# Products behind six norms start from the high parts alone, and a third weight panel is mixed into four of them

## Chip, cores and metric

The kernel runs on one core of one Trainium2 chip. The metric is the device time of one execution in microseconds, the median of three runs. Times from the trace are microseconds (us) of one profiled execution.

## What is computed

Two transformer blocks of depth 2 in a row, on 512 tokens of width 1024 (and 256 context tokens in the first block), all in float32 with float32 accuracy:

```python
# first block, for each of two layers (mixer A, then mixer B)
h  = rmsnorm(x, g) * (1 + scale) + shift      # likewise hc from the context
x  = x + gate * mixer(h, hc)
...
x  = rmsnorm(x, final_g)                      # norm "nf"
# second block, for each of two layers
y = rms_norm(h, nw[0])                        # norm "s00" (layer 0), "s10" (layer 1)
y = even_mixer(y) if layer == 0 else odd_mixer(y)
h = h + rms_norm(y, nw[1])                    # post norm "s01", "s11"
y = conv_ffn(rms_norm(h, nw[2]))              # norm "s02", "s12"
h = h + rms_norm(y, nw[3])                    # post norm "s03", "s13"
```

A `conv_ffn` is two products of 1024 x 2816 (`u`, `v`), a causal convolution of width 3 over `u`, `gelu(conv) * v`, and a product back to 1024.

## The kernel before

**Split products.** TensorE multiplies in a format with fewer mantissa bits than float32. Each operand is split in two parts of that format, `high = round(a)` and `low = a - high`, and a product is made of three: high x high, high x low, low x high (`split_product`, lines 364 to 366). For an activation the parts are `HH` and `HL`, in eight chunks k of 128 rows by 512 tokens; for a weight they are `WH` and `WL`. A weight panel is 1024 rows by 128 columns, eight chunks as well, so a panel with one output bank takes 24 matmuls of 512 columns.

**Who does what.** SyncE loads raw panels into three slots `raww`, in the order of use. ScalarE writes `WH` (`ahead`, line 307, instruction on line 316), GpSimd subtracts and writes `WL` (`split_low`, instruction on line 1449). There are three slots of `WH`/`WL` (`SPLIT = 3`, line 31): the high part of a panel can be written only after the last product of the panel three before it. All engines work strictly in program order, so `ahead` and `split_low` stand at places written out by hand in each engine's program, and a wait there holds everything behind it. The panels behind a norm are numbered here 0, 1, 2, 3 and so on in their order of use.

**The norms that the change touches.** Norms `n0` and `n1` (first block) scale before the product: VectorE makes `SQ` (line 2343), ScalarE rounds it into `HH` (lines 2097, 2098), VectorE subtracts into `HL` (line 2354), and signals `h_made`. The four "late" norms `s00`, `s02`, `s10`, `s12` multiply the product's result by the reciprocal root afterwards, so that products can start before the sum of squares is known. For each chunk k:

- VectorE finishes the residual `XC` chunk k. Behind a post norm this is `post_norm` (line 2363): L2368 scales `y` (mark `ynormed`), L2373 adds it to `XC` (mark `x_made`), L485 (`late_low`) makes `HL`. The loop is skewed: in step k it scales chunk k, adds chunk k-1, makes the low part of chunk k-2. For `s00` the loop is another (L2277, then `late_low` of chunk k-1), which the change leaves alone.
- ScalarE (`late_parts_act`, line 462) waits for `x_made`, writes `HH` chunk k (L466) and the square of the chunk into one of four places of `TMP` (L470). From k = 4 on the square waits for `statted[st, 3]`, TensorE's use of the first four squares, and the high parts of the later chunks stand behind it in the queue.
- TensorE (`lin_pair`, line 1555) takes two panels at once: for each k it waits for `h_made` (the low part) and issues the three products for each panel. After k = 3 and k = 7 it sums four squares (`square_group`, line 441, eight matmuls L447).

Behind the pair TensorE takes panel 2 by itself (`lin`, 24 matmuls), then `late_stat` (line 451, eight matmuls L455 of one column), which waits for ScalarE's copy of the sums (L472, mark `ss`), then panel 3, then `late_spread` (L515). This is so in `even_pe` (panels `e_f` 0 to 3), `ffn_pe` (`up_u` 0, `up_v` 0, `up_u` 1, `up_v` 1) and `odd_pe` (`o_k` 0 to 3). On ScalarE the copy `ss` is the last line of `late_parts_act`; the next line of its program is `ahead(act, ..., 4)`, which writes the high parts of panels 3 and 4 (`ffn_act`, line 2138, and the like in the other stages). The high part of panel 2 is written before the norm. GpSimd's low parts follow the high parts in order.

**PSUM banks** for products are handed out in turn, seven of them (`lin_bank`), and `claim` waits for the last reader of a bank.

## Time and profile before

| | us |
|---|---|
| median of 3 runs | 2239.02 (2236.71 to 2241.35) |
| profiled execution | 2237.86 |
| its span, first to last instruction | 2235.9 |
| TensorE busy | 2096.1 (94% of the span) |
| VectorE, ScalarE, GpSimd busy | 1042.0, 883.7, 724.7 |
| mean granted TensorE clock | 0.973 of full |

The time of a run holds the span and some 2 us around it. The page's fourth part follows the chain of work that ended last back through the engines: 82% of it is TensorE, 8% VectorE, 4% ScalarE. Its second part has a line PEclk, the clock that TensorE was granted in tenths of full speed. It is below 9 in three of the 40 slices, of 56 us each. A busy TensorE at half clock does half the work.

In the rows below, a name such as `L364` is a line of the kernel; `x8` behind a row is the number of instructions merged into it; the part in brackets is how long the engine had been idle, and whom it waited for.

### The profile page before, as it was taken

To read this page: it belongs to the slowest core of one execution; us is meant where nothing else is said; L and a number is where in the kernel's file an instruction comes from. 1 tells how busy PE (TensorE), PEld (TensorE's weight loads), DVE (VectorE), ACT (ScalarE), POOL (GpSimd) and SP (SyncE) were. 2 spreads that over 40 slices of the span, in tenths; PEclk is the share of its full clock that TensorE was granted. 3 is DMA by queue.
4 is the path that set the end of the run, shared out by engine and by line. 5 is a ranking of instruction groups with operands and counts; after the bars stand their busy time and mean duration, and the time that the engine had idled before them with its cause. 6 is when DMAs were issued, how large, how long until landed. Compare 5 with 4: busy or idle time off the path is not lost.

```text
span 2235.9 us, 29867 instructions
## 1 busy us (share of the span) xinstructions
PE 2096.1 (94%) x11466; PEld 1641.1 (73%) x11466; DVE 1042.0 (47%) x1722; ACT 883.7 (40%) x1636; POOL 724.7 (32%) x424
## 2 busy tenths in 40 slices
PE   5999999999999998998889999998998899999997
PEld 4888655788665645987667888886986677888886
DVE  3521887432466623377436434333127616625353
ACT  4322666433566723534443222234117723323222
POOL 1331122433000012240234444453444452444443
PEclk9999999999999999798989999999999999999999
DMA  7221333132000012220123333332331031333332
GB/s 282 66 67 57 105 100 91 48 104 72 14 1 1 1 48 65 67 87 28 41 64 94 104 94 93 102 89 76 95 95 34 25 104 50 110 94 92 106 90 71
DMA packets 255889, 169.16 MB, mean 76 GB/s; under 512 B 5776, under 2 KB 247159, under 8 KB 254599
## 3 DMA queue, kind: packets, MB, share of 16 engines
q1 hardware_dynamic: 252512, 158.55, 23.9%
q0 software_dynamic: 2192, 8.45, 1.2%
q8 instruction: 94, 1.54, 0.3%
q10 hardware_dynamic: 1047, 0.26, 0.1%
q14 instruction: 44, 0.36, 0.0%
HBM read 165.10 MB, written 2.14 MB: 75 GB/s over the span
## 4 chain that ended last, share of the span: by engine, by line
PE 82%; DVE 8%; issue 4%; ACT 4%; POOL 1%; DMA 0%; ACTq 0%; DVEq 0%; POOLq 0%
PE ps L364 20%; PE ps L366 20%; PE ps L365 20%; PE ps L542 6%; PE ps L650 5%; PE ps L614 3%; PE ps L1551 2%; PE ps L593 1%; DVE PT L632 1%; DVE MX L555 1%; POOL WL L1449 1%; DVE NB L552 1%; PE ps L982 1%; PE ps L515 1%; ACT PB L567 1%
## 5 line engine op out<-in xcount | busy, mean ns | idle before, releaser
L1449 POOL TENSOR_TENSOR WL<-raww,WH 128x1024 fp32r<-128x1024 f32 (+2 forms) x239 | 563.4, 2362 | 890.8 <-ACT WH L316 885.6
L364 PE MATMUL ps<-HH,WH 128*128 128x512 f32 (+1 forms) x1368 | 526.4, 385 | 31.6 <-DVE HL L485 19.5
L365 PE MATMUL ps<-HL,WH 128*128 128x512 f32 (+1 forms) x1368 | 521.0, 381 | 0.0
L366 PE MATMUL ps<-HH,WL 128*128 128x512 f32 (+1 forms) x1368 | 520.3, 380 | 0.0
L316 ACT ACTIVATE WH<-raww 128x1024 fp32r<-128x1024 f32 (+2 forms) x239 | 245.6, 1034 | 327.7 <-PE ps L366 327.6
L364 PEld LDWEIGHTS ps<-HH,WH 128*128 128x128 f32 x1368 | 261.2, 191 | 91.4 <-issue 28.0
L366 PEld LDWEIGHTS ps<-HH,WL 128*128 128x128 f32 x1368 | 260.6, 190 | 49.3
L365 PEld LDWEIGHTS ps<-HL,WH 128*128 128x128 f32 x1368 | 261.3, 191 | 46.9
L567 ACT ACTIVATE PB<-ps,NB 128x256 f32<-128x256 f32 (+5 forms) x256 | 168.1, 657 | 99.8 <-DVE NB L556 49.3
L614 PE MATMUL ps<-ident,PB 128*128 128x128 f32 x952 | 154.4, 278 | 11.6 <-DVE PT L632 7.1
L650 PE MATMUL ps<-PT,ARENA 128*64 128x512 f32 (+3 forms) x688 | 131.7, 490 | 10.0 <-ACT PT L634 6.5
L364 PE MATMUL ps<-f_h,WH 128*128 128x512 f32 x352 | 137.7, 391 | 1.6 <-DVE f_l L2571 1.6
L366 PE MATMUL ps<-f_h,WL 128*128 128x512 f32 x352 | 137.1, 389 | 0.0
L365 PE MATMUL ps<-f_l,WH 128*128 128x512 f32 x352 | 137.0, 389 | 0.0
L552 DVE TENSOR_REDUCE NB<-ps 128x1 f32<-128x768 f32 (+4 forms) x128 | 92.5, 723 | 93.2 <-PE ps L542 91.7
L614 PEld LDWEIGHTS ps<-ident,PB 128*128 128x128 f32 x952 | 108.7, 143 | 21.9 <-DVE PT L632 12.6
L634 ACT ACTIVATE PT<-ps 128x256 f32<-128x256 f32 (+1 forms) x192 | 83.7, 436 | 89.4 <-PE ps L614 87.2
L2384 DVE TENSOR_TENSOR ARENA<-ps,ARENA 128x512 f32<-128x512 f32 x60 | 40.9, 690 | 157.8 <-PE ps L366 131.0
L2558 DVE SCALAR_TENSOR_TENSOR ARENA<-ARENA,COL 128x511 f32<-128x511 f32 x44 | 110.8, 2519 | 1.6
L2147 ACT ACTIVATE ARENA<-ARENA 128x512 f32<-128x512 f32 x44 | 27.8, 632 | 172.9 <-DVE ARENA L2560 172.9
L555 DVE TENSOR_REDUCE MX<-ps 128x1 f32<-128x512 f32 (+3 forms) x128 | 74.1, 579 | 42.4 <-PE ps L542 42.0
L632 DVE COPY PT<-ps 128x384 f32<-128x384 f32 (+2 forms) x192 | 91.3, 476 | 3.2 <-PE ps L614 2.1
(324 smaller groups left out, 3344.1 us busy)
## 6 DMA issues: line engine op xcount, KB each, us to landing
raww<-in_ffn_w_up SPq DMA_DIRECT2D x88, 512.0 KB, 3.8
raww<-in_ada_w SPq DMA_DIRECT2D x32, 512.0 KB, 3.6
raww<-in_ffn_w_down SPq DMA_DIRECT2D x32, 448.0 KB, 3.7
raww<-in_odd_w_in SPq DMA_DIRECT2D x24, 512.0 KB, 3.7
raww<-in_even_w_in SPq DMA_DIRECT2D x21, 512.0 KB, 3.7
raww<-in_a_w_in SPq DMA_DIRECT2D x20, 512.0 KB, 3.8
raww<-in_ffn_w_down SPq DMA_DIRECT2D x16, 512.0 KB, 3.9
ADA<-in_ada_w SPq DMA_DIRECT2D x6, 1024.0 KB, 16.4
```

The costliest lines, as they stand in the source:

```text
L316: nc.scalar.activation(parts_of(k)[0], raw_slot(k), ACT.Copy).then_inc(*split_hi.mark(k))
L364: nc.tensor.matmul(out, lh, rh, start=start and k == ks[0], stop=False)
L365: nc.tensor.matmul(out, lh, rl, start=False, stop=False)
L366: ins = nc.tensor.matmul(out, ll, rh, start=False, stop=stop and k == ks[-1])
L542: ins = nc.tensor.matmul(ps[:, bk, c0 % 512:c0 % 512 + w], lhs, rhs, start=(q == 0), stop=(q == len(ms) - 1), skip_group_check=True)
L552: nc.vector.tensor_reduce(nb, score_span(A, r, i), AX_X, ALU.max, negate=True)\
L567: nc.scalar.activation(PB[:, t % 4, 0:job["tiles"][i]["n"] * P], score_span(A, r, i), ACT.Exp, bias=NB[:, r % 4, i:i + 1], scale=A["scale" ...
L614: ins = nc.tensor.transpose(ps[:, b, q * P:(q + 1) * P], PB[:, t % 4, (first + q) * P:(first + q + 1) * P], ident[:, :])
L632: nc.vector.tensor_copy(dst, src).then_inc(*pt_dve.mark(*key))
L650: ins = nc.tensor.matmul(ps[p0:p0 + HD, 7, a:z], v, PT[at][:, blk, q0_ + a:q0_ + z], start=(q == 0), stop=(q == n - 1), skip_group_check=True)
L1449: nc.gpsimd.tensor_tensor(lo, raw_slot(k), hi.bitcast(F32), ALU.subtract).then_inc(*split_lo.mark(k))
L2558: chain(dve, dve_step, nc.vector.scalar_tensor_tensor(c[:, 1:S], u[:, 0:S - 1], col(cw, 22 + m), c[:, 1:S], ALU.mult, ALU.add))
```

## The change

In `lin_pair` TensorE waits for the high part of chunk k (`act_out["hh", ...]`), issues the two products that use it for each panel, then waits for the low part (`h_made`) and issues the third. For the four late norms a third panel (panel 2) is mixed in: its chunks 0 to 3 follow the pair's chunks 1 to 4, its chunks 4 to 7 follow the pair's chunk 7. `square_group(..., 1)` stands behind all three panels, and `late_stat` right behind that. In `late_parts_act` all eight high parts come ahead of the squares 4 to 7. In `post_norm` the skew is one step less: the loop scales chunk k, makes the low part of chunk k-1, waits for the scaled chunk k and adds it. `ahead`, `split_low`, `late_stat`, `square_group` and the order of the panels stay as they are.

```diff
--- before.py
+++ after.py
@@ -465,8 +465,10 @@
                 act.wait_ge(*ready(k))
                 nc.scalar.activation(HH[:, k, 0:S], XC[:, k, 0:S], ACT.Copy, scale=col("norm_w_2", 8 * w + k))\
                     .then_inc(*act_out.mark("hh", st, k))
-                if k >= 4:
-                    act.wait_ge(*statted[st, 3])
+                if k < 4:
+                    nc.scalar.activation(TMP[:, k, :], XC[:, k, 0:S], ACT.Square).then_inc(*squared.mark(st, k))
+            act.wait_ge(*statted[st, 3])
+            for k in range(4, 8):
                 nc.scalar.activation(TMP[:, k % 4, :], XC[:, k, 0:S], ACT.Square).then_inc(*squared.mark(st, k))
             act.wait_ge(*statted[st, 7])
             nc.scalar.activation(TMP[:, 0, :], bank(("ss", st)), ACT.Copy).then_inc(*act_out.mark("ss", st))
@@ -1552,26 +1554,49 @@
                 ins.then_inc(*grouped.mark(*gk))
             last_use(key, *gk)
 
-        def lin_pair(pe, two, h_, segs, ready, st=None):
-
-            outs = []
-            for stage, key, m, reader_of in two:
-                pe.wait_ge(*split_lo[key,])
+        def lin_pair(pe, two, h_, segs, norm, st=None, third=None):
+
+            def claimed(stage, key, m, reader_of):
                 for name, r0, nr in segs:
                     b = lin_bank((stage, m, name))
                     claim(pe, b, reader_of(m, name))
-                    outs.append((stage, key, m, name, r0, nr, b))
-            for k in range(8):
-                pe.wait_ge(*ready(k))
+                    yield stage, key, m, name, r0, nr, b
+
+            def step(outs, k, low_made=None):
                 for stage, key, m, name, r0, nr, b in outs:
                     wh, wl = parts_of(key)
-                    ins = split_product(ps[:, b, 0:nr], lambda k: (wh[:, k, :], wl[:, k, :]), h_(r0, nr), [k],
-                                        k == 0, k == 7)
+                    hh, _ = h_(r0, nr)(k)
+                    nc.tensor.matmul(ps[:, b, 0:nr], wh[:, k, :], hh, start=(k == 0), stop=False)
+                    nc.tensor.matmul(ps[:, b, 0:nr], wl[:, k, :], hh, start=False, stop=False)
+                if low_made:
+                    pe.wait_ge(*low_made)
+                for stage, key, m, name, r0, nr, b in outs:
+                    wh, _ = parts_of(key)
+                    _, hl = h_(r0, nr)(k)
+                    ins = nc.tensor.matmul(ps[:, b, 0:nr], wh[:, k, :], hl, start=False, stop=(k == 7))
                     if k == 7:
                         ins.then_inc(*grouped.mark(stage, m, name))
-                if st and k % 4 == 3:
-                    square_group(pe, st, k // 4)
-            for stage, key, m, _ in two:
+
+            outs, late, late_k = [], [], 0
+            for one in two:
+                pe.wait_ge(*split_lo[one[1],])
+                outs += claimed(*one)
+            for k in range(8):
+                pe.wait_ge(*act_out["hh", norm, k])
+                step(outs, k, h_made[norm, k])
+                if third and 1 <= k <= 4:
+                    if k == 1:
+                        pe.wait_ge(*split_lo[third[1],])
+                        late += claimed(*third)
+                    step(late, late_k)
+                    late_k += 1
+                if st and k == 3:
+                    square_group(pe, st, 0)
+            for k in range(late_k, 8 if third else 0):
+                step(late, k)
+            if st:
+                square_group(pe, st, 1)
+            for stage, key, m, _ in two + ([third] if third else []):
                 last_use(key, stage, m, segs[-1][0])
 
         def lin_rows(pe, stage, name, c, nn, tiles, reader):
@@ -1599,7 +1624,7 @@
         def mixer_a_pe(pe):
             lin_pair(pe, [("ak", ("a_k", m), m,
                            lambda m, s: (act_out, ("raw", "ak", m)) if s == "lat" else (act_out, ("akc", m)))
-                          for m in range(2)], h_at, BOTH, lambda k: h_made["n0", k])
+                          for m in range(2)], h_at, BOTH, "n0")
             lin_rows(pe, "av", "a_v", 0, 256, range(6), lambda t: (act_out, ("av", t)))
             for m in range(8):
                 lin(pe, "aq", ("a_q", m), m, h_at, BOTH,
@@ -1615,7 +1640,7 @@
 
             lin_pair(pe, [("ckv", ("b_ckv", 0), 0, lambda m, s: (act_out, ("ckv", s))),
                           ("kr", ("b_kr", 0), 0, lambda m, s: (act_out, ("kr", s)))], h_at, BOTH,
-                     lambda k: h_made["n1", k])
+                     "n1")
             for m in range(2):
                 lin(pe, "cq", ("b_cq", m), m, h_at, LAT, lambda m, s: (act_out, ("cq", m)))
 
@@ -1655,11 +1680,9 @@
 
         def even_pe(pe):
             lin_pair(pe, [("ef", ("e_f", m), m, lambda m, s: (dve_out, ("efr", m))) for m in range(2)], h_at, LAT,
-                     lambda k: h_made["s00", k], "s00")
-            for m in range(2, 4):
-                lin(pe, "ef", ("e_f", m), m, h_at, LAT, lambda m, s: (dve_out, ("efr", m)))
-                if m == 2:
-                    late_stat(pe, "s00")
+                     "s00", "s00", ("ef", ("e_f", 2), 2, lambda m, s: (dve_out, ("efr", m))))
+            late_stat(pe, "s00")
+            lin(pe, "ef", ("e_f", 3), 3, h_at, LAT, lambda m, s: (dve_out, ("efr", m)))
             late_spread(pe, "s00")
             lin_rows(pe, "ev", "e_v", 0, P, range(4), lambda t: (act_out, ("ev", t)))
             for i in range(2):
@@ -1812,12 +1835,13 @@
                 if what == "up" and i == 0:
                     lin_pair(pe, [(f"u{l}", ("up_u", l, 0), 0, lambda m, s: (dve_out, ("u", l, m))),
                                   (f"v{l}", ("up_v", l, 0), 0, lambda m, s: (dve_out, ("prod", l, m)))], h_at, LAT,
-                             lambda k: h_made[before, k], before)
+                             before, before,
+                             (f"u{l}", ("up_u", l, 1), 1, lambda m, s: (dve_out, ("u", l, m))))
+                    late_stat(pe, before)
                     continue
                 if what == "up":
-                    lin(pe, f"u{l}", ("up_u", l, i), i, h_at, LAT, lambda m, s: (dve_out, ("u", l, m)))
-                    if i == 1:
-                        late_stat(pe, before)
+                    if i > 1:
+                        lin(pe, f"u{l}", ("up_u", l, i), i, h_at, LAT, lambda m, s: (dve_out, ("u", l, m)))
                     lin(pe, f"v{l}", ("up_v", l, i), i, h_at, LAT, lambda m, s: (dve_out, ("prod", l, m)))
                     if i == 1:
                         late_spread(pe, before)
@@ -1844,11 +1868,10 @@
 
         def odd_pe(pe):
             lin_pair(pe, [("ok", ("o_k", m), m, lambda m, s: (dve_out, ("ok", m))) for m in range(2)], h_at, LAT,
-                     lambda k: h_made["s10", k], "s10")
-            for m in range(2, 8):
+                     "s10", "s10", ("ok", ("o_k", 2), 2, lambda m, s: (dve_out, ("ok", m))))
+            late_stat(pe, "s10")
+            for m in range(3, 8):
                 lin(pe, "ok", ("o_k", m), m, h_at, LAT, lambda m, s: (dve_out, ("ok", m)))
-                if m == 2:
-                    late_stat(pe, "s10")
                 if m == 3:
                     late_spread(pe, "s10")
             for i in range(4):
@@ -2363,17 +2386,17 @@
         def post_norm(dve, st, w, nxt):
             norm_recip(dve, st, 4)
             dve.wait_ge(*rinv_made[st, 0])
-            for k in range(10):
+            for k in range(9):
                 if k < 8:
                     nc.vector.scalar_tensor_tensor(y_of[st][:, k, :], y_of[st][:, k, :], col("norm_w_2", 8 * w + k),
                                                    bank(("rinv", st, 0)), ALU.mult, ALU.mult)\
                         .then_inc(*dve_out.mark("ynormed", st, k))
-                if 1 <= k < 9:
-                    dve.wait_ge(*dve_out["ynormed", st, k - 1])
-                    nc.vector.tensor_tensor(XC[:, k - 1, 0:S], XC[:, k - 1, 0:S], y_of[st][:, k - 1, :], ALU.add)\
-                        .then_inc(*x_made.mark(st, k - 1))
-                if k >= 2:
-                    late_low(dve, nxt, k - 2, w + 1)
+                if k >= 1:
+                    late_low(dve, nxt, k - 1, w + 1)
+                if k < 8:
+                    dve.wait_ge(*dve_out["ynormed", st, k])
+                    nc.vector.tensor_tensor(XC[:, k, 0:S], XC[:, k, 0:S], y_of[st][:, k, :], ALU.add)\
+                        .then_inc(*x_made.mark(st, k))
             late_recip(dve, nxt)
 
         def late_scaled(dve, dst, key, done, st, by=None):
```

## Rows read from the trace of the kernel before

**Rows 1.** Page, parts 1 and 2: busy us of each engine; granted TensorE clock in tenths.

```profile
PE 2096.1 (94%) x11466; PEld 1641.1 (73%) x11466; DVE 1042.0 (47%) x1722; ACT 883.7 (40%) x1636; POOL 724.7 (32%) x424
...
PEclk9999999999999999798989999999999999999999
```

**Rows 2.** Waits of TensorE, whole run: us in total, times, longest us.

```profile
PE ps L364 <- DVE HL L485: 19.5, 8, 5.0
...
PE ps L364 <- DVE HL L2354: 7.8, 2, 4.1
...
PE ps L364 <- POOL WL L1449: 3.9, 5, 1.5
```

**Rows 3.** Timeline, norm n1: start us, us, engine, line, what, count, [idle before, releaser].

```profile
492.23 0.49 ACT L2098 ACTIVATE HH<-SQ,MODS 128x256 fp32r<-128x256 f32 x1
...
494.05 0.76 PE L364 MATMUL ps<-HH,WH 128*128 128x512 f32 x1 [3.66 <-DVE HL L2354]
```

**Rows 4.** Timeline, first products behind norm s02.

```profile
1149.91 1.41 DVE L2368 SCALAR_TENSOR_TENSOR ARENA<-ARENA,COL,ps 128x512 f32<-128x512 f32 x2 [2.17 <-PE ps L515]
1151.23 0.69 DVE L2373 TENSOR_TENSOR XC<-XC,ARENA 128x512 f32<-128x512 f32 x1
...
1151.95 0.72 ACT L466 ACTIVATE HH<-XC,COL 128x512 fp32r<-128x512 f32 x1 [4.42 <-DVE XC L2373]
...
1153.10 0.74 DVE L485 SCALAR_TENSOR_TENSOR HL<-XC,COL,HH 128x512 fp32r<-128x512 f32 x1
...
1153.98 0.77 PE L364 MATMUL ps<-HH,WH 128*128 128x512 f32 x1 [4.12 <-DVE HL L485]
...
1155.02 0.74 DVE L485 SCALAR_TENSOR_TENSOR HL<-XC,COL,HH 128x512 fp32r<-128x512 f32 x1
...
1155.68 0.74 DVE L2368 SCALAR_TENSOR_TENSOR ARENA<-ARENA,COL,ps 128x512 f32<-128x512 f32 x1
```

**Rows 5.** Timeline, norm s02 behind the first four squares, chunk 5.

```profile
1164.56 0.75 DVE L485 SCALAR_TENSOR_TENSOR HL<-XC,COL,HH 128x512 fp32r<-128x512 f32 x1 [1.77 <-ACT HH L466]
...
1165.37 0.50 PE L364 MATMUL ps<-HH,WH 128*128 128x512 f32 x1 [0.56 <-DVE HL L485]
```

**Rows 6.** Timeline, norm s02 from the last four squares to the fourth panel.

```profile
1169.67 1.06 PE L447 MATMUL ps<-TMP,ones 128*32 128x512 f32 x8
...
1170.80 0.60 ACT L472 ACTIVATE TMP<-ps 128x512 f32<-128x512 f32 x1 [3.48 <-PE ps L447]
...
1172.43 4.75 POOL L1449 TENSOR_TENSOR WL<-raww,WH 128x1024 fp32r<-128x1024 f32 x2 [24.05 <-ACT WH L316]
...
1176.25 0.95 PE L455 MATMUL ps<-oned,TMP 128*128 128x1 f32 x8
...
1177.05 0.49 PE L364 MATMUL ps<-HH,WH 128*128 128x512 f32 x1
```

**Rows 7.** Timeline, first products behind norm s00.

```profile
864.88 7.45 POOL L1449 TENSOR_TENSOR WL<-raww,WH 128x1024 fp32r<-128x1024 f32 x3 [8.12 <-ACT WH L316]
...
870.25 0.76 PE L364 MATMUL ps<-HH,WH 128*128 128x512 f32 x1 [4.96 <-DVE HL L485]
```

**Rows 8.** Timeline of TensorE, one-column products with a wait among them, between 512-column ones.

```profile
534.17 1.39 PE L417 MATMUL ps<-oned,SQ 128*128 128x1 f32 x12
536.53 2.02 PE L417 MATMUL ps<-oned,SQ 128*128 128x1 f32 x16 [0.96 <-ACT SQ L395]
```

**Rows 9.** Stretches: us, busy us (count) of each engine, granted clock, DMA share, GB/s.

```profile
538.20:541.63 3.43, 3.43 (x11) 2.75 (x11) 0.00 (x0) 2.95 (x4) 0.00 (x0) 0.50 0.00 0
1153.98:1159.44 5.46, 5.46 (x13) 4.30 (x14) 5.46 (x9) 3.42 (x6) 0.00 (x0) 0.50 0.00 0
1845.68:1848.93 3.25, 3.25 (x8) 2.57 (x9) 3.25 (x6) 1.89 (x4) 0.00 (x0) 0.50 0.02 5
903.50:927.30 23.80, 23.80 (x114) 23.80 (x113) 5.68 (x15) 9.26 (x15) 4.22 (x3) 0.50 0.08 23
```

**Rows 10.** Timeline, entry of the e_v products.

```profile
902.55 0.30 PE L364 MATMUL ps<-WH,HH 128*128 128x128 f32 x1 [2.27 <-DVE ARENA L2384]
```

## The prediction

> **What bounds the kernel now.** I read the page's busy line first: TensorE is busy for 94% of the span, no other engine for half of it [rows 1]. What matters is therefore which stretches of TensorE's work move, where it stands still, and at which clock it runs. The list of TensorE's waits comes next: 19.5 us in eight waits for the low parts of the late norms and 7.8 us in two for those of n0 and n1 [rows 2]. These ten waits are the most that the change can touch. They are not all the low part's fault. Then I read the timeline at each norm. Behind s02 the first scaling starts at 1149.91, the sum is there at 1151.92, the high part at 1152.67, the low part at 1153.84, and the first product starts at 1153.98 [rows 4]. A second, short wait stands behind the first four squares, at chunk 5: 0.56 us, because the high part of chunk 5 stood behind a square on ScalarE [rows 5]. Last I read what happens between the last squares and panel 3, where the change takes work away [rows 6], and the granted clock of stretches, since TensorE comes out of these waits at 1.2 GHz: 13 products in 5.46 us, 0.42 us each, against 0.23 us at 2.4 GHz (24 products between the end of L447 at 1170.73 and 1176.25) [rows 6, 9].
>
> **Norms n0 and n1.** VectorE's and ScalarE's work stays; the first product waits for the high part. In n1 that ends at 492.72; with the 0.14 us from the end of a part to its product (1153.84 to 1153.98 in [rows 4]) TensorE starts at 492.86 and not at 494.05 [rows 3, 4]. Gain 1.2 us. n0 has the same two steps and a wait as long [rows 2], so 2.4 us for both. The same three products per panel and chunk are issued in another order: no cost. TensorE gets one wait more per chunk, 48 in all. At most chunk borders of today it passes a satisfied wait, and the list of waits shows no time for them, so I take nothing; the upper bound is 0.11 us each (a first product after a wait takes 0.50 us and not 0.39 [rows 5]), 5 us in all.
>
> **Head of the three post norms (s02, s10, s12).** Today the first high part is the third link: two scalings, one addition. In the changed order it is scaling 0.74, addition 0.69, high part 0.72, with 0.03 us between engines (1151.92 to 1151.95) and 0.14 to TensorE: 2.35 us behind 1149.91, against 4.07 today [rows 4]. Gain 1.7 us each. The new order on VectorE is slower per chunk, though. Today a cycle takes 1.92 us (low part at 1153.10, the next at 1155.02). Now the low part of a chunk waits for the high part of the same chunk and holds up the next addition: 0.68 + 0.03 + 0.72 + 0.03 from the start of an addition to the start of the low part, 0.66 more to the next addition (1155.02 to 1155.68), 2.1 us [rows 4]. The last low part is there 18.0 us behind 1149.91. TensorE still needs 2 + 12 products and the squares after it, 4.3 us, so it can't be done before 22.3; by its own work it is done 26.3 us behind today (1176.25), less the gains here, 23.9. The supply does not bind, but it caps the gain at 4.0 us where the clock should rise early. Panel 2 covers this: with it a chunk costs 9 x 0.23 = 2.1 us, the pair alone 1.4.
>
> **Chunk 5 (all four late norms).** The high parts run ahead of the squares, so the wait of 0.56 us and the 0.11 us of its first product go: 0.7 us each [rows 5]. The squares 4 to 7 come later on ScalarE but still before panel 2 is done: nothing.
>
> **Head of s00.** Here two low weight parts have to be ready. Three take 7.45 us from 864.88, so the second is there near 869.85; the first product starts at 870.25 today and at 869.95 then: 0.3 us [rows 7]. Panel 2's low part ends at 872.3, before TensorE is through chunk 1.
>
> **Panel 3: a new wait.** This term decides. Today the chain behind the last squares is: L447 at 1169.67, copy of the sums on ScalarE 1170.80, behind it in ScalarE's queue the high part of panel 3, then GpSimd's low part from 1172.43, the first of two in 4.75 us, so until 1174.80 [rows 6]. Meanwhile TensorE does panel 2's 24 products (5.5 us) and the eight small ones of L455, so it never waits for that chain. The change moves those 24 products ahead of the squares and leaves the chain as it is, hanging on the squares. Now L455 waits for the copy (end 1.73 us behind the start of L447, where L447 ends at 1.06), and panel 3 waits for its low part, 5.14 us behind it; with the step to TensorE 5.2. Today's distance from L447 to panel 3 is 1177.05 - 1169.67 = 7.4, of which 5.5 is panel 2. So 5.2 stands where 1.9 would be: +3.3 us at each of four norms, +13.2 us. Who else waits: on TensorE everything; the low part of panel 4 and the later ones keep their distance to panel 3 and have slack. I see no bound much below this, since each link is a queue order that the diff doesn't touch; 2.9 to 3.6.
>
> **The clock in the new wait.** TensorE now has 512-column products, then 0.7 us of nothing, 0.8 us of one-column products and 2.6 us of nothing. The nearest row is a stretch from 534.17 to 538.4 with only one-column products and a wait of 0.96 us; behind it the clock was 1.2 GHz for 3.4 us [rows 8, 9]. At half speed 3.4 us cost 1.7. Low stretches elsewhere last 3.25 to 5.46 us [rows 9]. I take 1.7 at each, +6.8; bounds 0 and 2.7. The Trainium skill speaks for the lower bound: its page "TensorE: Matmul & The Clock Gate", section "Why this matters for your kernels", only warns of idle gaps longer than either piece here. By it the clock stays and this term is nothing. The trace does not agree, as the stretch at 534 had no longer gap. The same page, Part 1, says that the number of slow products varies from run to run of one kernel; that agrees with the 3.25 and 5.46 us here, and is why I use a mean at the heads: starting 1.7 us earlier in the low state may give 0.85, or up to 3.4 where the rise comes a step earlier.
>
> **Banks.** Panel 2 now takes the bank before the sum of squares and not after. In the even stage the last bank that the e_v products claim is then read by the third of four L2384 and not the second, some 0.6 us later, on top of the wait of 2.27 us [rows 10]: +0.6. In the other stages these readers are long done.
>
> **Sum.** -2.4 (n0, n1) -5.1 (three heads) -0.3 (s00) -2.8 (chunk 5) +13.2 +6.8 +0.6 = +10.0 us. The profiled execution took 2237.9, so 2247.9; the median of the three runs is 1.1 above it, so 2249.0. Later waits (for instance 3.9 us for GpSimd's parts [rows 2]) hang on late_spread, which moves along, so nothing absorbs the shift.
>
> **Rivals.** (B) The stall is there, the clock stays up: 2249.0 - 6.8 = 2242.2, no measurable change. For it: the two idle pieces are short, and this is what the skill's rule above would give. Against it: [rows 8, 9].
> (C) Not slower, by the clock at one place: the e_v products run at 1.2 GHz for 23.8 us behind the wait of 2.27 us [rows 9, 10]. Should the clock stay up there, half of that, 11.9, comes back: 2237. It decides if the clock does not fall in 902 to 904. Against it: the wait before it grows by 0.6, and the work that follows is the same 128-column kind.
> (D) Panel 3's parts are ready by another way and only the gains are left: -10.6 + 0.6, 2229. That needs a high part ahead of the copy of the sums on ScalarE, which the order of its program forbids; it would also be the case if I misread that order.
> (E) The 48 added waits cost 0.11 us each and low stretches last longer: 2254 and above. Against it: the satisfied waits of today.
>
> **Chances.** Forecast 0.60 (2245 to 2254 with the bounds of head, clock and stall), B 0.15, C 0.08, D 0.08, E 0.09. A measurement of this kernel can tell about 0.2%, 4.5 us. D is faster (0.08); B and C are the same (0.23); forecast and E slower (0.69). The range takes in the forecast, B and most of C, and leaves out D and half of E: 2238 to 2254.
>
> **What would show it.** Right: TensorE's waits for L485 and L2354 shrink from 27.3 us by some 12; new waits of L455 for L472 (0.7 us, four) and of L364 for L1449 (2.6 us, four) appear; low clock behind each; VectorE's cycle is 2.1 us. Wrong: panel 3's first product less than 5 us behind the last L447, or a granted clock of 1.00 through these stretches, or e_v products at 2.4 GHz.

## The result, and the profile after

The changed kernel takes 2254.99 us (median of 4 runs, 2251.12 to 2256.05), the kernel before 2239.39 us beside it: ratio 1.0064, 95% interval 1.0049 to 1.0078, so 15.6 us slower. The forecast was 2249.0, 10 us slower. The median lies 1 us above the upper end of the range. The profiled execution took 2254.13 us; its span is 2252.2 us against 2235.9 before, 16.3 more.

TensorE's waits of the changed kernel, whole run (us in total, times, longest; late_low is now L487, the low weights L1451, the copy of the sums L474, the products of a pair L1569, L1570 and L1576):

```profile
PE ps L364 <- POOL WL L1451: 13.0, 9, 2.3
...
PE ps L1569 <- ACT HH L466: 7.2, 3, 2.4
...
PE ps L1569 <- ACT HH L2121: 5.4, 2, 3.0
PE ps L1569 <- POOL WL L1451: 4.5, 1, 4.5
...
PE ps L364 <- ACT TMP L1892: 3.6, 1, 3.6
PE ps L455 <- ACT TMP L474: 3.2, 4, 0.8
...
PE ps L364 <- DVE ARENA L2407: 2.9, 1, 2.9
```

The 27.3 us of waits for low parts in [rows 2] are now 17.1 us, for high parts and, at s00, for a low weight panel (7.2 + 5.4 + 4.5). In return the wait of L364 for GpSimd's weights rose from 3.9 to 13.0 us, and a new wait of 3.2 us stands ahead of L455. Of both kinds one new wait stands at the same place of each late norm. Timeline at the head of s02, which answers to [rows 4]:

```profile
1161.69 0.75 DVE L487 SCALAR_TENSOR_TENSOR HL<-XC,COL,HH 128x512 fp32r<-128x512 f32 x1
...
1161.80 0.77 PE L1569 MATMUL ps<-HH,WH 128*128 128x512 f32 x1 [2.41 <-ACT HH L466]
...
1163.83 0.75 DVE L487 SCALAR_TENSOR_TENSOR HL<-XC,COL,HH 128x512 fp32r<-128x512 f32 x1
```

The first product no longer waits for the low part, and VectorE's cycle is 2.14 us for a chunk (1161.69 to 1163.83). Timeline behind the last squares of s02 (start us, us, engine, line; idle before and its releaser in brackets), which answers to [rows 6]:

```profile
1181.41 1.06 PE L447 MATMUL ps<-TMP,ones 128*32 128x512 f32 x8
1182.55 0.60 ACT L474 ACTIVATE TMP<-ps 128x512 f32<-128x512 f32 x1 [3.79 <-PE ps L447]
1183.04 1.99 ACT L316 ACTIVATE WH<-raww 128x1024 fp32r<-128x1024 f32 x2
1183.29 1.02 PE L455 MATMUL ps<-oned,TMP 128*128 128x1 f32 x8 [0.81 <-ACT TMP L474]
1184.16 4.68 POOL L1451 TENSOR_TENSOR WL<-raww,WH 128x1024 fp32r<-128x1024 f32 x2 [26.28 <-ACT WH L316]
...
1186.57 0.79 PE L364 MATMUL ps<-HH,WH 128*128 128x512 f32 x1 [2.26 <-POOL WL L1451]
```

Follow one release after another: squares on TensorE, copy on ScalarE, high weights behind it in ScalarE's queue, low weights on GpSimd, product on TensorE. Between the squares and that product TensorE has only the eight small products of L455 in its program, so it stands still for the rest of the chain. From the squares to the fourth panel (the prediction's panel 3) it is 5.16 us.

Four stretches of the changed kernel, with the columns of [rows 9]: behind that stall, the rest of the panel, behind s00's stall, and the entry of the e_v products. The column in front of the last two numbers is the granted clock:

```profile
1186.30:1189.71 3.41, 3.14 (x8) 2.48 (x8) 0.32 (x2) 0.00 (x0) 3.41 (x3) 0.50 0.52 148
1189.72:1193.50 3.78, 3.78 (x18) 3.13 (x17) 0.00 (x0) 0.00 (x0) 1.47 (x1) 1.00 0.69 201
...
896.10:902.90 6.80, 5.91 (x14) 4.65 (x15) 0.94 (x2) 0.00 (x0) 3.29 (x3) 0.50 0.65 203
909.80:933.60 23.80, 23.80 (x114) 23.80 (x114) 5.06 (x13) 8.21 (x13) 3.17 (x3) 0.50 0.08 23
```

The clock is 1.2 GHz (0.50) behind the stall of s02 for 3.4 us, and behind that of s00 for 6.8.

The next table lays out each late norm by stages: from the spread that precedes it to the first product of the pair, on to L455, to the fourth panel, and to the norm's own spread. Times are us, between starts in TensorE's timelines of both kernels. In both, the stretch to L455 holds 72 products and both groups of squares; in the changed kernel it also holds the new wait of 0.81.

| norm | to the first product | to L455 | to the fourth panel | to its spread | sum |
|---|---|---|---|---|---|
| s00 | 6.12, now 5.64 | 22.59, now 20.98 | 0.81, now 3.28 | 5.58, now 8.38 | +3.16 |
| s02 | 6.19, now 4.49 | 22.26, now 21.49 | 0.81, now 3.28 | 5.58, now 7.02 | +1.44 |
| s10 | 5.81, now 4.49 | 22.03, now 21.97 | 0.81, now 3.28 | 5.59, now 7.18 | +2.69 |
| s12 | 6.19, now 4.49 | 21.36, now 21.70 | 0.81, now 3.28 | 5.58, now 7.15 | +2.67 |

The four norms make +10.0 us of the +16.3. Of the rest, 3.0 us are there before s00 begins and 3.4 come between s00 and s02.

### The profile page after: what moved, and what is told of

Its sections match the earlier page's. It is cut to its first block, busy times and chain, and to the rows that moved or that the text cites. A ratio compares the mean times of both kernels' runs of the same rounds, so it can differ in the third digit from the quotient of the medians.

```text
span 2252.2 us, 29867 instructions
## 1 busy us (share of the span) xinstructions
PE 2110.1 (94%) x11466; PEld 1653.9 (73%) x11466; DVE 1052.4 (47%) x1722; ACT 883.7 (39%) x1636; POOL 723.1 (32%) x424
## 3 DMA queue, kind: packets, MB, share of 16 engines
HBM read 165.10 MB, written 2.14 MB: 74 GB/s over the span
## 4 chain that ended last, share of the span: by engine, by line
PE 74%; issue 12%; DVE 7%; POOL 3%; ACT 3%; DMA 0%; ACTq 0%; DVEq 0%; POOLq 0%
PE ps L364 17%; PE ps L365 17%; PE ps L366 17%; PE ps L544 6%; PE ps L652 5%; PE ps L616 3%; POOL WL L1451 2%; PE ps L1553 2%; PE ps L595 1%; DVE PT L634 1%; DVE MX L557 1%; POOL ACC L378 1%; DVE NB L554 1%; PE ps L984 1%; ACT PB L569 1%
## 5 line engine op out<-in xcount | busy, mean ns | idle before, releaser
L1451 POOL TENSOR_TENSOR WL<-raww,WH 128x1024 fp32r<-128x1024 f32 (+2 forms) x239 | 562.6, 2359 | 906.4 <-ACT WH L316 901.2
L364 PE MATMUL ps<-HH,WH 128*128 128x512 f32 (+1 forms) x1208 | 463.0, 383 | 13.3 <-POOL WL L1451 12.8
L365 PE MATMUL ps<-HL,WH 128*128 128x512 f32 (+1 forms) x1208 | 460.1, 381 | 0.0
L366 PE MATMUL ps<-HH,WL 128*128 128x512 f32 (+1 forms) x1208 | 459.5, 380 | 0.0
L364 PEld LDWEIGHTS ps<-HH,WH 128*128 128x128 f32 x1208 | 229.6, 190 | 58.1 <-POOL WL L1451 14.8
L366 PEld LDWEIGHTS ps<-HH,WL 128*128 128x128 f32 x1208 | 229.4, 190 | 43.4
L365 PEld LDWEIGHTS ps<-HL,WH 128*128 128x128 f32 x1208 | 229.7, 190 | 42.2
L364 PE MATMUL ps<-f_h,WH 128*128 128x512 f32 x352 | 137.7, 391 | 1.6 <-DVE f_l L2594 1.6
```

The source lines that it names most:

```text
L364: nc.tensor.matmul(out, lh, rh, start=start and k == ks[0], stop=False)
L365: nc.tensor.matmul(out, lh, rl, start=False, stop=False)
L366: ins = nc.tensor.matmul(out, ll, rh, start=False, stop=stop and k == ks[-1])
L1451: nc.gpsimd.tensor_tensor(lo, raw_slot(k), hi.bitcast(F32), ALU.subtract).then_inc(*split_lo.mark(k))
```

## Experiments

Each kernel was run 5 to 12 times beside the kernel before (the changed kernel 4 times). In the table "norms" is the sum over the four late norms, from the preceding spread to the norm's own, read off each kernel's trace as above, less the 138.1 us of the kernel before. "Median" is the difference from the median of the kernel before that ran beside it. A trace is one execution: those of e1_no_third, e5_head_filler and p2_high_first_act_order are the slowest of theirs, 3.8 to 5.3 us above their medians, so a difference of a microsecond or two between two traces settles nothing by itself.

| kernel | ratio, 95% interval | median, us | norms, us |
|---|---|---|---|
| changed kernel | 1.0064, 1.0049 to 1.0078 | +15.6 | +10.0 |
| e1_no_third | 0.9999, 0.9990 to 1.0007 | -1.3 | -3.3 |
| e2_squares_early | 0.9980, 0.9971 to 0.9988 | -5.0 | -8.6 |
| e3_first_block_old | 1.0060, 1.0048 to 1.0072 | +13.3 | +8.8 |
| e4_filler | 1.0034, 1.0022 to 1.0046 | +7.4 | +7.4 |
| p1_high_first | 0.9978, 0.9969 to 0.9987 | -5.2 | -7.8 |
| p4_third_only | 1.0086, 1.0073 to 1.0099 | +19.1 | +17.7 |
| e5_head_filler | 0.9974, 0.9963 to 0.9985 | -6.0 | -7.9 |
| e7_dve_old | 0.9985, 0.9977 to 0.9994 | -3.1 | -5.5 |
| e6_squares_early_first_old | 0.9963, 0.9951 to 0.9976 | -8.1 | -8.6 |
| e8_early_dve_old_filler | 0.9963, 0.9951 to 0.9976 | -7.9 | -9.9 |
| e9_high_first_filler | 0.9977, 0.9967 to 0.9988 | -5.7 | -9.4 |
| p2_high_first_act_order | 0.9976, 0.9965 to 0.9987 | -6.0 | -8.4 |

### The third panel by itself again

```diff
-                     "s00", "s00", ("ef", ("e_f", 2), 2, lambda m, s: (dve_out, ("efr", m))))
+                     "s00", "s00")
+            lin(pe, "ef", ("e_f", 2), 2, h_at, LAT, lambda m, s: (dve_out, ("efr", m)))
             late_stat(pe, "s00")
```

and the same in the other two stages.

> The changed kernel, but the third panel is not mixed in: its 24 products come by themselves behind the last squares, as before the change. High parts first and both new orders stay. If the stall ahead of the next panel, and the low clock behind it, are what made the kernel slower, both are gone: the wait of that panel's first product for its low weights falls from 3.2 to nearly 0 at four places (about 13 us), and the four clock falls (3.4 to 6.8 us of 1.2 GHz each) go with it. Time 2230 to 2237 us, 18 to 25 below the changed kernel and a few below the kernel before. The rival, that the 48 added waits or the order of the other products cost as such, gives 2250 or more.

Measured: 2237.94 us, 0.9 above the expected range. The wait of L364 for L1451 is back at 4.0 us in five (3.9 before), the one of L455 is gone, the fourth panel follows L455 at 0.81, and there is no low clock behind it. So the stall and its clock belong to the mixed panel: 17 us by the medians. A few us below the kernel before were expected, and the two can't be told apart: most of the gains at the three heads are gone too. Its timeline at s02 shows where to:

```profile
1169.23 0.50 PE L1569 MATMUL ps<-HH,WH 128*128 128x512 f32 x1 [0.47 <-ACT HH L466]
1171.37 0.51 PE L1569 MATMUL ps<-HH,WH 128*128 128x512 f32 x1 [0.48 <-ACT HH L466]
1173.46 1.07 PE L447 MATMUL ps<-TMP,ones 128*32 128x512 f32 x8 [0.41 <-ACT TMP L472]
```

With 48 products and not 72 ahead of the last squares, TensorE catches up with the row of chunks on VectorE, now 2.14 us each, and waits at the last two chunks and at the squares. The pair starts 1.7 us earlier behind its spread, and L455 comes 1.3 us later behind the first product.

### The last squares ahead of the rest of the third panel

```diff
+            if st:
+                square_group(pe, st, 1)
             for k in range(late_k, 8 if third else 0):
                 step(late, k)
-            if st:
-                square_group(pe, st, 1)
```

> The changed kernel, but the last squares come ahead of the third panel's four remaining steps (12 products, 2.7 us) instead of behind them; nothing is left out. By the theory of the chain (sum on ScalarE, high and low weights of the next panel, 5.2 us from the squares), the stall shrinks by the 2.7 us that these products now cover: 0.4 to 0.8 us for the first product of the fourth panel where it was 2.2 to 3.5, the wait of the spread squares for the copy of the sum goes. About 11 us less by waits, and up to 7 less by the clock if it no longer falls: 2238 to 2246 us. By the rival in which mixing or added waits cost as such, it stays within 2 us of the changed kernel.

Measured: 2234.24 us, 21 us below the changed kernel and 5 below the kernel before. Its timeline at s02:

```profile
1172.61 1.06 PE L447 MATMUL ps<-TMP,ones 128*32 128x512 f32 x8
...
1173.74 0.60 ACT L474 ACTIVATE TMP<-ps 128x512 f32<-128x512 f32 x1 [1.64 <-PE ps L447]
...
1175.37 4.72 POOL L1451 TENSOR_TENSOR WL<-raww,WH 128x1024 fp32r<-128x1024 f32 x2 [24.12 <-ACT WH L316]
...
1176.47 0.95 PE L455 MATMUL ps<-oned,TMP 128*128 128x1 f32 x8
...
1177.80 0.50 PE L364 MATMUL ps<-HH,WH 128*128 128x512 f32 x1 [0.38 <-POOL WL L1451]
```

The stretch behind it, with the columns of the stretches above:

```profile
1178.00:1183.30 5.30, 5.30 (x24) 4.37 (x24) 2.19 (x2) 0.67 (x1) 4.43 (x2) 1.00 0.66 196
```

The chain is as long as before (1172.61 to 1177.80, 5.19 us), but twelve products run inside it, the wait shrinks from 0.81 + 2.26 to 0.38, and the clock stays at 2.4 GHz behind it. Behind so short a wait the clock fell at none of the four norms. The expectation's two sums, 11 for the waits and 7 for the clock, make 18 us against the changed kernel; the norms of the two traces differ by 18.5, and the other 2 us of the 21 lie outside the norms. The place of the last squares was the whole loss.

### Keeping TensorE busy in the stall

```diff
+        def fill(pe, n, key):
+            b = LIN[turn["lin"] % turn["banks"]]
+            for sgn, at in readers[b]:
+                pe.wait_ge(*sgn[at])
+            for i in range(n):
+                nc.tensor.matmul(ps[:, b, :], ident[:, :], XC[:, i % 8, 0:S], start=True, stop=True)
         def late_stat(pe, st):
+            fill(pe, 1, st)
             ...
+            fill(pe, 4, st)
```

> The changed kernel with products added whose results nobody reads (identity by activations in 32 bit, 512 columns, into a bank that is free): one ahead of the sum product of each late norm and four behind it, where the engine would wait for the next panel's weights. The stall is a wait for other engines, so these add nothing as long as they fit into it (about 3 us). If the low clock behind the stall comes from TensorE's idleness, it stays at 2.4 GHz there, and the time falls by 4 to 7 us against the changed kernel, to 2248 to 2251. If the clock falls for another cause, the time is unchanged or, where the added products outlast the stall, up to 4 us longer.

The first block defines the added products; one stands ahead of L455's and four behind them (`...` marks the lines of `late_stat` between).

Measured: 2246.64 us, 8.4 below the changed kernel and 1.4 below the expected range, with twenty more products of 512 columns. At s02 (added products at L457; L455 is now L464):

```profile
1176.24 0.95 PE L464 MATMUL ps<-oned,TMP 128*128 128x1 f32 x8
1177.05 3.68 PE L457 MATMUL ps<-XC,ident 128*128 128x512 f32 x8
```

The stretch from there to the spread:

```profile
1177.05:1186.00 8.95, 8.95 (x34) 6.10 (x34) 1.41 (x2) 1.95 (x3) 7.03 (x3) 1.00 0.48 134
```

The granted clock is 1.00 where it was 0.50 for 3.4 us (6.8 at s00), at all four norms. So the low clock behind the stall comes from TensorE's idleness in it. Through L455 and the fourth panel to the spread it takes 9.81 us against 10.30 of the changed kernel. By the trace the four norms give back only 2.5 us. The stretch from the fourth panel to the spread was 1.4 to 2.8 us longer in the changed kernel than in the kernel before, 7.4 at four norms, and this low clock is gone. But the added products outlast the stall: the fourth panel comes 3.93 us behind L455's products and not 3.28, and the spread 5.88 behind the panel and not 5.58, 3.8 us at four norms; the stretches to L455 are 1.1 us longer as well. 7.4 - 3.8 - 1.1 is the 2.5. The rest of the 8.4 has its place outside the norms, where no product was added, in stretches whose clock differs between the traces (below).

### One part of the change at a time, on the kernel before

p1_high_first takes from the diff only the high parts first at the late norms. p4_third_only takes only the mixed panel (each step then issues all three products behind the wait for its low part, as before). The comments in brackets stand for code.

```diff
 # p1_high_first, step of lin_pair at a late norm, against the kernel before
-                pe.wait_ge(*ready(k))
+                pe.wait_ge(*act_out["hh", norm, k])
+                (HH x WH and HH x WL of both outputs)
+                pe.wait_ge(*h_made[norm, k])
+                (HL x WH of both outputs)
 # p4_third_only
+                if third and 1 <= k <= 4:
+                    step(late, late_k)
...
+            for k in range(late_k, 8 if third else 0):
+                step(late, k)
             if st:
                 square_group(pe, st, 1)
```

> The kernel before, with one part of the change alone: at the four late norms each step's products with the high part are issued ahead of a wait for the low part. Orders on ScalarE and VectorE and the panels are as before. The first product then starts about 1 us earlier at each of three heads (and 0.5 at the one of s00). If this is kept up to the last squares, the time is 3 to 4 us below the kernel before (2235 to 2236). The rival: the last squares hang on VectorE's and ScalarE's row of chunks and not on TensorE, so the products catch up with it and wait there; the time is then within 1 us of the kernel before.

> The kernel before, with another part alone: the third panel mixed in between the steps and ahead of the last squares, everything else as before. If this part alone carries the cost, the chain from the last squares to the fourth panel stands bare here too: 3.3 us of waits at each of four places and 1.5 of low clock behind, about 18 to 20 us, against which stands a wait of 0.6 at chunk 5 that the mixed products hide: 2254 to 2259. If the cost needs the new orders or the added waits, this kernel is at 2240 to 2248.

Measured: 2234.68 and 2259.01 us. One part gains 5.2 us, the other costs 19.1. By the four norms of their traces it is -7.8 and +17.7, which sum to +9.9, and the changed kernel has +10.0; the closeness is in part chance, since neither kernel has the new orders on ScalarE and VectorE, and the one on VectorE is not free (below). The stall stands bare in p4_third_only, with the old orders and without the added waits:

```profile
PE ps L364 <- DVE HL L485: 16.4, 4, 4.1
PE ps L364 <- POOL WL L1449: 13.0, 9, 2.3
...
PE ps L455 <- ACT TMP L472: 3.2, 4, 0.8
```

### The two norm pairs of the first block

e3_first_block_old is the changed kernel and e6_squares_early_first_old the one with the squares early, both with the n0 and n1 pairs waiting for both parts at each step:

```diff
-            lin_pair(pe, [("ak", ("a_k", m), m,
+            first_pair(pe, [("ak", ("a_k", m), m,
                 ...
-                          for m in range(2)], h_at, BOTH, "n0")
+                          for m in range(2)], h_at, BOTH, lambda k: h_made["n0", k])
```

> The changed kernel, but the two norm pairs of the first block go as before the change (each step waits for both parts of its input, high and low products together). The four late norms keep the change. The trace of the changed kernel has these pairs begin 1.2 us earlier, but the products of the next stage wait 1.0 us longer for the copies of the pair, and three low stretches of the clock lie in this block where one lay before. If that clock belongs to the change, this kernel is 1 to 3 us faster than the changed one; if the clock there is chance, it is 0 to 0.5 us slower.

> The kernel with the last squares early (label e2_squares_early), with the two norm pairs of the first block as before the change. Over five traces the products of the late norms are reached 1.5 to 1.9 us later than in the kernel before where these pairs are old, and -0.1 to 2.5 later where they are new. So the new pairs are worth 0.3 us, not the 2.4 forecast: 2234 to 2236. If the 2.4 was there and clock chance hid it, this kernel is at 2237; if the new pairs cost, as the median with the label e3_first_block_old would have it, it is at 2232.

Measured: 2252.59 us (changed kernel 2254.99) and 2232.32 us (with new pairs 2234.24). Both are some 2 us faster with the old pairs. The intervals of each couple overlap, so a cost is not shown. A gain of 2.4 us would put the ratio with new pairs 0.0011 below the other; it lies 0.0004 and 0.0017 above, and the second couple, with half intervals of 0.0012 and 0.0009, rules such a gain out. The traces agree: the spread ahead of s00 starts at 865.4 to 868.5 us in the seven with new pairs, 866.8 on average, and at 865.6 to 867.6 in the six others with old ones, 866.7 on average.

Timeline of the changed kernel behind n0, its first product and the first of a_v:

```profile
45.45 0.47 PE L1569 MATMUL ps<-HH,WH 128*128 128x512 f32 x1 [2.96 <-ACT HH L2121]
...
67.50 0.55 PE L364 MATMUL ps<-WH,HH 128*128 128x256 f32 x1 [3.56 <-ACT TMP L1892]
```

The pair starts 1.39 us earlier than before (46.84), but the a_v products only 0.48 earlier (67.98): they wait 3.56 us for the copies of the pair's outputs where they waited 2.62. Then the clock is at 1.2 GHz for 6.8 us in the changed kernel, as it is with the old pairs of e3_first_block_old, and was not in the trace of the kernel before; so this low stretch is not the new pairs' doing. One row of each, the changed kernel first:

```profile
66.70:73.50 6.80, 6.00 (x28) 6.03 (x29) 6.70 (x6) 3.00 (x6) 5.21 (x2) 0.50 0.27 77
```

e3_first_block_old:

```profile
67.80:74.60 6.80, 6.12 (x29) 6.16 (x30) 6.70 (x6) 2.88 (x6) 5.09 (x2) 0.50 0.26 77
```

The kernel before:

```profile
66.70:73.00 6.30, 5.02 (x42) 5.05 (x43) 6.26 (x4) 3.46 (x7) 5.12 (x2) 1.00 0.31 85
```

### VectorE's order, and the clock at the heads

e7_dve_old is e2_squares_early with the loop of post_norm as before the change (scaling k, addition k - 1, low part k - 2). e5_head_filler is e2_squares_early with unread products around the spread:

```diff
+            fill(pe, 4)
             norm_spread(pe, after, 4, (dve_out, ("ynormed", after, 7)))
+            fill(pe, 8)
```

e8_early_dve_old_filler has both, e9_high_first_filler is p1_high_first with the added products, and p2_high_first_act_order is p1_high_first with ScalarE's new order.

```diff
 # e7_dve_old: post_norm
-            for k in range(9):
+            for k in range(10):
                 (scaling of chunk k)
-                if k >= 1:
-                    late_low(dve, nxt, k - 1, w + 1)
-                (addition of chunk k)
+                (addition of chunk k - 1)
+                if k >= 2:
+                    late_low(dve, nxt, k - 2, w + 1)
 # p2_high_first_act_order: late_parts_act
-                if k >= 4:
-                    act.wait_ge(*statted[st, 3])
-                (square of chunk k)
+                if k < 4:
+                    (square of chunk k)
+            act.wait_ge(*statted[st, 3])
+            (squares of chunks 4 to 7)
```

> The kernel with the last squares early (label e2_squares_early), with VectorE's order of the post-norm as before the change: the low part of a chunk comes one chunk later, and the adds wait for nothing that ran just before them. VectorE's row then takes 1.92 us for a chunk where the new order takes 2.14 (1.7 us for eight), but the first chunk of x comes 0.65 later. If VectorE's row sets the last squares, this is 1 us quicker at each of three heads: 2231. If TensorE's 72 products do, it loses the 0.65 three times: 2236.

> The kernel with the last squares early (label e2_squares_early), plus products whose results nobody reads (identity by identity, 32 bit, 128 columns) at the three heads behind a post-norm: four ahead of the spread of the reciprocals, eight behind it, where TensorE has 1.7 and 2.4 us idle. They add no work to the path if they fit. The head's products run at 1.2 GHz for about 10 us in every trace so far. If that clock comes from the idleness ahead, it stays at 2.4 GHz, and the spread (2.07 us for 1.05) and the first products are quicker: 1 to 2 us at each of three heads, 2228 to 2232. If VectorE's row of chunks (2.14 us each) sets the head whatever the clock, only the quicker spread is won: 2231 to 2234. If the added products push the spread back, it is slower than the kernel without them.

> The kernel with the last squares early, with VectorE's old order of the post-norm (label e7_dve_old) and with the products at the head whose results nobody reads (label e5_head_filler). Theory: the head is set by the slower of two rows, VectorE's chunks (2.14 us each in the new order, 1.92 in the old) and TensorE's products, which a clock of 1.2 GHz for 10 us lengthens by 2 to 2.5. Either cure alone gained nothing. Both together should gain 8 times 0.22 less 0.5 for the later first chunk, 1.2 us at each of three heads, against either: 2230 to 2232. If either row alone is the bound, it stays at 2234 to 2237.

> The kernel with high parts first alone (label p1_high_first), plus the same products at the three heads whose results nobody reads. There TensorE waits for nothing between the first product of the pair and the last squares, and has 3.6 to 5.2 us at 1.2 GHz in that stretch, which costs 1.8 to 2.6. If the clock is kept up, TensorE gives back what the VectorE and ScalarE rows allow, 1 to 1.8 us at each of three heads: 2229 to 2232. If these rows are as late already, it stays at 2234.

> The kernel with high parts first alone (label p1_high_first), plus ScalarE's new order: all high parts ahead of the last four squares. The last squares then follow the eighth high part, which hangs on VectorE's row of 1.92 us a chunk, with 2.2 us of four squares behind it, where the old order had squared three of the four chunks by then. 0.5 us later at each of three heads: 2235 to 2237. If the early high parts help the products (they wait for nothing in the trace of the other), it is at 2233 or less.

Measured: 2236.74, 2233.90, 2232.52, 2234.64 and 2234.37 us. With the added products the granted clock is 1.00 from the first product of the pair to L455 at s02, s10 and s12, where it was 0.50 for 3.5 to 5.2 us; in e5_head_filler the sum from spread to spread is 32.1 to 32.3 us against 31.7 to 32.7 in e2_squares_early: no gain. TensorE is faster there and waits for VectorE's row instead (e5_head_filler, at s02):

```profile
1170.88 0.50 PE L1579 MATMUL ps<-HH,WH 128*128 128x512 f32 x1 [0.25 <-ACT HH L474]
1172.97 1.07 PE L447 MATMUL ps<-TMP,ones 128*32 128x512 f32 x8 [0.43 <-ACT TMP L480]
```

The old order alone is slower (32.7 to 33.3; the first product comes 5.0 us behind the spread at s02 and s12, not 4.5, and TensorE's own work at low clock binds). Both together (e8_early_dve_old_filler) give 31.6 at each of the three, on average 1.5 less than e7_dve_old and 0.6 less than e5_head_filler; 1.2 against either was expected. By the ratios e8_early_dve_old_filler is clear of e7_dve_old and not of e5_head_filler. So two rows of about equal length, VectorE's and TensorE's, end at the last squares: the added products gain nothing with VectorE's new order and 1.5 us a head with the old one. e9_high_first_filler, with clock 1.00 at the three heads, has 31.7 to 32.3 there, 0.4 a head below p1_high_first, and the medians show no gain (-5.7 and -5.2), where 1 to 1.8 a head was expected. ScalarE's new order changes nothing beside p1_high_first (32.2 to 32.7 and 32.2 to 32.8): the forecast half microsecond is not there.

What VectorE's new order is worth thus depends on the panel. With the third panel mixed in it gains a little (e2_squares_early against e7_dve_old, -2.5 over the three heads, -1.9 by the median differences of the table; their intervals overlap, so this rests on the traces). With 48 products alone ahead of the last squares it loses (e1_no_third against p2_high_first_act_order, +5.4 over the three heads and +4.7 by the table, where the intervals are apart; the second figure has the first block's pairs in it).

The fastest kernels are e6_squares_early_first_old and e8_early_dve_old_filler, at 0.9963 of the kernel before; they can't be told apart, and the first does it without added work.

## Why the prediction was right in sign and short in size

**Panel 3, +13.2.** Right. Measured per norm: the wait of L455 is 0.81, and the fourth panel comes 3.28 behind L455 and not 0.81, together +3.3; +13.1 at four. The distance to the panel is 5.16 us for 5.2. e1_no_third, e2_squares_early and p4_third_only each tie it to the mixed panel and to its place ahead of the squares.

**The clock in the new wait, +6.8.** Right in mechanism: 3.4 us at 1.2 GHz behind three of the stalls and 6.8 behind s00's. By the stretch to the spread it cost 2.8 + 1.4 + 1.6 + 1.6 = 7.4. e4_filler shows the cause, idleness: with the pieces filled the low clock is gone at all four norms. Rival B (clock stays up) fell. The Trainium skill, in "TensorE: Matmul & The Clock Gate", section "Why this matters for your kernels", warns only of idle gaps longer than about 3 us. The gaps here are 0.81 and 2.26 us, with 1.0 us of one-column products between them, and the clock fell all the same, so the measurement decides against reading that warning as a promise for shorter gaps.

**Heads, -5.1 and -0.3.** Right. The first product came 1.70, 1.32 and 1.70 us earlier behind its spread and 0.48 at s00: -4.7 and -0.5. VectorE's cycle is 2.14 us for the 2.1 forecast. "The supply does not bind" held only because the third panel's products were in between; e1_no_third shows it binding with 48 products, and e5_head_filler with 72 at full clock.

**Chunk 5, -2.8.** The wait of 0.56 stood at all four norms of the kernel before and at none of the changed kernel. The stretch to L455, without the new wait of 0.81 in it, is 2.4, 1.6, 0.9 and 0.5 us shorter: -5.4 and not -2.8. In it 19.5 us were at low clock before (5.9, 5.5, 4.9 and 3.2) and 16.4 after (2.9, 4.0, 5.0 and 4.5), which at half speed is 1.6 of the 5.4; the prediction took nothing for the clock here. The other 1.0 can't be placed.

**Banks, +0.6.** Right: the wait at e_v is 2.91 for 2.27, and e_v runs at 1.2 GHz for 23.8 us as before. Rival C fell.

**Norms n0 and n1, -2.4.** This step failed. "VectorE's and ScalarE's work stays; the first product waits for the high part" was right, the start 1.4 us earlier at n0. But I stopped at the first product and did not follow the end: at n0 the next products wait for the copies of the pair's outputs (3.56 us, for 2.62 before), and 0.48 us of 1.39 is left at a_v. By the runs the two pairs bring nothing or cost 2 us.

**The rest.** The terms of the late norms and the banks were forecast at +12.4 and measured at +10.6 in the trace. The size was missed elsewhere: 2.4 to 4.4 us for n0 and n1, and the clock outside the norms, a term that the prediction put at nothing. The granted clock of each run, averaged over its span, is on record: 0.964 to 0.966 in the four runs of the changed kernel, 0.969 to 0.974 in those of the kernel before. As twice the missing share of the span, an estimate, that is 158 us at 1.2 GHz against 125 in the median. By the traces the four norms, from spread to spread, hold 50.9 and 41.6 of it. Some 24 us more thus lie outside them, 10 ahead of s00, 10 between s00 and s02 and 4 between s10 and s12.

The largest piece is behind the s00 norm, in attention of the even stage (1040 to 1110): 23.9 us at 1.2 GHz before and 34.1 after, while the lag between the traces grows there by 2.7 us. No part of the change touches this code, and over the fourteen traces the number does not follow the time: 20.5 with p4_third_only and 34.1 with p2_high_first_act_order, whose medians are 25 us apart in the other direction. But it is not chance of one trace alone either: with e4_filler the clock is 0.972 to 0.973 in all five runs, and outside the norms its trace has 17 us less at 1.2 GHz than the changed kernel's. Why the clock outside the norms goes with the kernel stays open.

The trace of the kernel before is short outside the norms, 2097.7 us where the thirteen others have 2099.0 to 2106.5. It is so already ahead of s00, by 1.5 to 3.5 us against the six kernels whose program is the same up to there, and the time of this profiled execution is 1.5 below the kernel's median. In the table above the median lies 0.0 to 5.6 us above the change of the four norms, 2.5 on average, with old and with new pairs alike. If these 2.5 are put down to the one trace that all share, the changed kernel would stand at 12.5; this is an estimate, and no run tests it. 3 us of its +15.6 stay without a cause even so.

**Rivals D and E.** D (only gains are left) did not come; it is what e2_squares_early makes of the change, at -5.0 us and not -10. E (added waits cost as such) fell: p1_high_first has 32 of the 48, is faster than the kernel before, and its pair at s02 runs from the first product to the last squares without a wait.

## What to carry to other kernels

A block of independent work that stands behind a signal to other engines is often the cover for their answer. Before it is moved ahead, measure the chain from the signal to the next thing that this engine needs, and leave at least so much of the block behind the signal: here twelve of 24 products made the difference between 16 us lost and 5 us won. An earlier start counts only up to the next place where the work of several engines meets, so follow it to there before it is booked as a gain.

## What the runs showed of the hardware

- The clock fell to 1.2 GHz behind two idle pieces of 0.81 and 2.26 us with 1.0 us of one-column products between them (four of four norms), and stayed at 2.4 GHz behind a single one of 0.38 us (e2_squares_early, four of four) and where added 32-bit products filled the pieces (e4_filler, four of four).
- A low stretch at the same place of the same code lasted 3.4 us in some traces and 6.8 in others (three places in the attention of the even stage, before and after the change; behind the stall of s00, 3.4 in e3_first_block_old and 6.8 in the changed kernel). Over the runs of one kernel, the kernel before, the mean granted clock went from 0.969 to 0.974 and the time from 2234.2 to 2243.1 us. A single pair of traces can misplace a few us.
- Unread products that kept the clock at 2.4 GHz for a whole head did not shorten it (32.2 us from spread to spread on average in e5_head_filler, 32.2 in e2_squares_early): here a low clock cost nothing, because VectorE's row was as long. With VectorE's row shorter (e8_early_dve_old_filler against e7_dve_old) they gained 1.5 us a head.
